# An encoder layer's down projection: staggered by sequence over its last chunks, with its half switch bank by bank and layer norm 2 spread out

## The reference

```
hdn = dwconv_centred(x @ ffn_w_up, ffn_conv_w) + ffn_conv_b
gate, val = split(hdn, 2)                       # 2816 columns each
ffn = (silu(gate) * val) @ ffn_w_down           # 2816 -> 1024
y = layer_norm(ALPHA * x + ffn, ln2_g, ln2_b)   # over the 1024 channels
```

## Time and profile before

| | |
|---|---|
| median of three runs | 1607.79 us (1606.72 to 1609.69) |
| span of the profiled execution | 1607.6 us |
| the median less that span | 0.2 us |
| TensorE, matmuls | 1456.8 us busy, 91% of the span |
| VectorE | 934.6 us, 58% |
| ScalarE | 501.1 us, 31% |
| GpSimd | 495.5 us, 31% |
| chain of waits, by engine | TensorE 70%, VectorE 21%, ScalarE 3% |

### The profile page before, as it was taken

One profiled execution on the slowest core, in us unless ns is written; L12 is line 12 of the kernel. 1 busy time (PEld: TensorE's weight loads), 2 busy tenths in 40 slices (PEclk: granted clock), 3 DMA queues, 4 the chain that ended last, 5 costly groups with the idle time before them and its releaser, 6 DMA issues.

```text
span 1607.6 us, 20068 instructions
## 1 busy us (share of the span) xinstructions
PE 1456.8 (91%) x7078; PEld 1179.5 (73%) x7078; DVE 934.6 (58%) x1447; ACT 501.1 (31%) x906; POOL 495.5 (31%) x235
## 2 busy tenths in 40 slices
PE   7999999798898897889579999999999999996992
PEld 5777767686786786768348888888888888875871
DVE  4344458858859779669884444434444445258337
ACT  4333346155163263421252212222221211212125
POOL 4322212112112122025254434434433444533323
PEclk9999999899899998999889999999999999998996
DMA  7110101100101001001001111111111111111002
GB/s 225 40 40 27 40 14 32 40 14 32 26 14 44 13 27 45 1 27 53 26 13 48 44 52 52 39 52 52 39 52 52 43 49 52 42 50 34 31 14 105
DMA packets 44326, 68.18 MB, mean 42 GB/s; under 512 B 24048, under 2 KB 26736, under 8 KB 44272
## 3 DMA queue, kind: packets, MB, share of 16 engines
q1 hardware_dynamic: 43696, 66.46, 13.1%
q10 hardware_dynamic: 576, 1.05, 0.2%
HBM read 62.00 MB, written 5.51 MB: 42 GB/s over the span
## 4 chain that ended last, share of the span: by engine, by line
PE 70%; DVE 21%; issue 4%; ACT 3%; DMA 2%; DVEq 0%; SPq 0%; POOL 0%; ACTq 0%
PE banks L503 33%; PE banks L955 14%; PE banks L528 11%; DVE qkv L1539 2%; DVE outer L1605 1%; PE banks L636 1%; PE banks L792 1%; PE banks L872 1%; DVE mix L1846 1%; DVE mix L1775 1%; PE banks L658 1%; DVE inv L1608 1%; DVE d_n L1699 1%; PE banks L646 1%; DVE sum L1788 1%
## 5 line engine op out<-in xcount | busy, mean ns | idle before, releaser
L441 POOL TENSOR_TENSOR w_hi<-w_raw,one 128x1024 fp32r<-128x1024 f32 (+1 forms) x103 | 196.0, 1903 | 1030.5 <-PE banks L503 496.8
L503 PE MATMUL banks<-x_hi,w_hi 128*128 128x512 f32 (+1 forms) x912 | 366.5, 402 | 30.5 <-POOL x_lo L463 16.9
L503 PE MATMUL banks<-x_hi,w_lo 128*128 128x512 f32 (+1 forms) x912 | 358.8, 393 | 0.0
L503 PE MATMUL banks<-x_lo,w_hi 128*128 128x512 f32 (+1 forms) x912 | 358.8, 393 | 0.0
L1870 DVE SCALAR_TENSOR_TENSOR cv<-banks,fw,cv 128x511 f32<-128x511 f32 x176 | 131.9, 750 | 260.6 <-ACT cv L1331 252.8
L444 POOL TENSOR_TENSOR w_lo<-w_raw,w_hi 128x1024 fp32r<-128x1024 f32 (+1 forms) x103 | 263.7, 2560 | 8.1
L503 PEld LDWEIGHTS banks<-x_hi,w_hi 128*128 128x128 f32 (+1 forms) x912 | 172.8, 189 | 77.6 <-POOL x_lo L463 20.6
L503 PEld LDWEIGHTS banks<-x_lo,w_hi 128*128 128x128 f32 (+1 forms) x912 | 172.8, 189 | 37.8 <-issue 2.8
L503 PEld LDWEIGHTS banks<-x_hi,w_lo 128*128 128x128 f32 (+1 forms) x912 | 172.3, 189 | 38.0 <-issue 0.6
L1331 ACT ACTIVATE cv<-banks,fw_j 128x512 f32<-128x512 f32 x88 | 68.7, 780 | 333.6 <-PE banks L503 331.1
L955 PE MATMUL banks<-a_hi,w_hi 128*128 128x512 f32 x352 | 139.7, 397 | 18.8 <-DVE a_lo L1898 15.6
(11 more groups left out here) (226 smaller groups left out, 2143.4 us busy)
## 6 DMA issues: line engine op xcount, KB each, us to landing
w_raw<-w_all SPq DMA_DIRECT2D x102, 512.0 KB, 3.3
yT<-z_all SPq DMA_DIRECT2D x16, 256.0 KB, 2.0
mix<-xT SPq DMA_DIRECT2D x12, 256.0 KB, 8.0
bw<-rpb SPq DMA_DIRECT2D x8, 132.5 KB, 12.0
mix<-xT ACTq DMA_DIRECT2D x4, 256.0 KB, 5.9
inverse_dram<-inv SPq DMA_DIRECT2D x4, 256.0 KB, 2.2
packed<-inverse_dram SPq DMA_DIRECT2D x16, 64.0 KB, 2.6
cst<-consts SPq DMA_DIRECT2D x1, 848.0 KB, 10.6
```

The source lines that it names most:

```text
L441: nc.gpsimd.tensor_tensor(w_hi[u][:, 0:n], w_raw[ru][:, 0:n], one[:, :].to_broadcast([P, n]), ALU.mult).then_inc(w_high, 1)
L503: last = mm(ps[bank][0:cols, :], w[u][:, k * cols:(k + 1) * cols], seq(x[:, k, :], s), start=n == 0, stop=n == 3 * KT - 1)
```

## The change

The first half keeps its order up to c10. The rest is rewritten:

- **Half switch.** c10 waits for both of its tiles and then finishes bank by bank (`half_finished`); VectorE reads each bank when it is done. The shift is summed from banks 0 and 1, after the first four banks. The two tiles of c11 stand in buffers of their own, in a part of `x_lo` that is no longer needed, since all rejoining of x (`joined`) is now done within the first half.
- **Moves.** A turn of the loop over c12 to c17 handles two chunks, and after each chunk's two `low` stands one group of four operations (`moved`): subtract the shift, scale block m + 4, add to the sum, add the square.
- **Stagger.** c18 to c21 (`STAG` = 4) are done for sequence 0 alone, all eight tiles, and then for sequence 1 bank by bank. All eight tiles' two parts (`h_last`, `l_last`) and four chunks' weights stay in memory for it; c20 and c21 have weight buffers of their own, for which GpSimd waits for no product. Sequence 0's sums (`stats2(0)`) stand after the first bank of sequence 1.
- **Layer norm 2.** Sequence 0's normalising is spread between the additions for sequence 1. The last tile of sequence 1 goes into the sums by matmuls of its own. The inverse root and the scaled mean that VectorE multiplies by stand in the PSUM banks `ps[4 + s]` and `ps[6 + s]`; GpSimd has copies in SBUF (`rs_row`, `mu_row`).

```diff
+        for u in range(2):
+            a_hi.append(x_lo[:, 2 * u, :])
+            a_lo.append(x_lo[:, 2 * u + 1, :])
...
+        h_last, late = place("h_last", [P, 2 * STAG, T], F32R, m)
+        w_late = []
+        for u in range(2):
+            t, late = place(f"w_hi_late{u}", [P, D], F32R, late)
+            t2, late = place(f"w_lo_late{u}", [P, D], F32R, late)
+            w_late.append((t, t2))
+        sq_last, late = place("sq_last", [P, L], F32, late)
+        rs_row, late = place("rs_row", [P, SEQS, L], F32, late)
+        assert late <= m + 2 * LONG * T * 4
+        l_last, _ = place("l_last", [P, 2 * STAG, T], F32R, m + 2 * LONG * T * 4)
...
-            split_chunks(UP0 + 3, CHUNKS)
+            split_chunks(UP0 + 3, DOWN0 + DPASS + 1)
+            split_chunks(DOWN0 + DPASS + 1, CHUNKS - 2, 6)
+
+            pool.wait_ge(a_ready, FJ + 12)
+            for u in range(2):
+                c = CHUNKS - 2 + u
+                split(c, raw(c), 3 + u, 16 * (c // 2 + 1), None)
...
+            def half_finished(c, w):
+                pe.wait_ge(w_ready, c + 1)
+                pe.wait_ge(a_ready, FJ)
+                for m in range(4):
+                    for s in range(SEQS):
+                        for t in range(2):
+                            ins = down_products(m, s, w, t, a_hi[t], a_lo[t], False, t == 1)
+                        ins.then_inc(proj_done, 1)
+                    if m == 1:
+                        pe.wait_ge(acc_read, SEQS)
+                        for s in range(SEQS):
+                            mm(ps[s][:, :], mean_w[:, :], seq(z_all[:, 0, :], s), start=True, stop=True
+                               ).then_inc(shift_summed2, 1)
...
+                pe.wait_ge(summed2, 2)
+                mm(ps[1][:, :], mean_w[:, :], sum2[:, 1, :], start=True, stop=False)
+                pe.wait_ge(sq_added2, 1 + 15)
+                mm(ps[3][:, :], mean_w[:, :], sumsq2[:, 1, :], start=True, stop=False)
+                pe.wait_ge(d_ready2, 16)
+                mm(ps[1][:, :], mean_w[:, :], seq(z_all[:, KT - 1, :], 1), start=False, stop=True)
+                pe.wait_ge(sq_last_ready, 1)
+                mm(ps[3][:, :], mean_w[:, :], sq_last[:, :], start=False, stop=True).then_inc(stats_done2, 1)
...
+            late = [(c0 + LONG + e, slot(c0 + LONG + e) if e < 2 else 1 + e) for e in range(STAG)]
+            for e, (c, w) in enumerate(late):
+                pe.wait_ge(w_ready, c + 1)
+                for t in range(2):
+                    n = 2 * e + t
+                    pe.wait_ge(a_ready, FJ + 2 * LONG + n + 1)
+                    for m in range(4):
+                        ins = down_products(m, 0, w, t, h_last[:, n, :], l_last[:, n, :], False, n == 2 * STAG - 1)
+                        if n == 2 * STAG - 1:
+                            ins.then_inc(proj_done, 1)
+            for m in range(4):
+                for e, (c, w) in enumerate(late):
                     for t in range(2):
+                        n = 2 * e + t
+                        ins = down_products(m, 1, w, t, h_last[:, n, :], l_last[:, n, :], False, n == 2 * STAG - 1)
+                ins.then_inc(proj_done, 1)
+                if m == 0:
+                    stats2(0)
+            stats2(1)
...
+            def root_rows(s):
+                act_e.wait_ge(stats_done2, s + 1)
+                A(sum2[:, s, :], ps[s][:, :], ACT.Square).then_inc(mean_squared, 1)
+                act_e.wait_ge(var_ready2, s + 1)
+                A(sumsq2[:, s, :], sumsq2[:, s, :], ACT.Ln, bias=eps[:, 2:3]).then_inc(ln_step2, 1)
+                act_e.wait_ge(ln_step2, s + 1)
+                A(rs_row[:, s, :], sumsq2[:, s, :], ACT.Exp, scale=-0.5).then_inc(rs_rows2, 1)
+                A(ps[4 + s][:, :], sumsq2[:, s, :], ACT.Exp, scale=-0.5).then_inc(rs_banked, 1)
+                act_e.wait_ge(mu_banked, s + 1)
+                nc.scalar.copy(mu_row[:, s, :], ps[6 + s][:, :]).then_inc(rows2_ready, 1)
...
+            def moved(m, s, n):
+                zt = tile_of(z_all, m, s)
+                TT(zt, zt, c2[:, s, :], ALU.subtract).then_inc(d_ready2, 1)
+                zt = tile_of(z_all, m + 4, s)
+                step(STT(zt, zt, ALPHA, c2[:, s, :], ALU.mult, ALU.subtract))
                 dve.wait_ge(d_ready2, n + 1)
-                return TT(sum2[:, s, :], sum2[:, s, :], tile_of(z_all, m, s), ALU.add)
+                step(TT(sum2[:, s, :], sum2[:, s, :], tile_of(z_all, m, s), ALU.add))
+                add_square2(n, s, s)
 
...
+            with dve.Fori(0, 3) as i:
+                step.enter(i, 2 * SEQS, base)
                 for s in range(SEQS):
+                    for u in range(2):
+                        t = 2 + 2 * s + u
+                        low(4 * i + (FJ + t), 4 * i + t, u)
+                    moved(i, s, 2 * i + s)
+            step.leave(3)
+            for n in range(2 * STAG):
+                dve.wait_ge(a_high, FJ + 2 * LONG + n + 1)
+                TT(l_last[:, n, :], act[:, 2 * LONG + n, :], h_last[:, n, :].bitcast(F32), ALU.subtract
+                   ).then_inc(a_ready, 1)
+                if n in (1, 3):
+                    moved(3, n // 2, 6 + n // 2)
...
+            def rows(s):
+                dve.wait_ge(mean_squared, s + 1)
+                TT(sumsq2[:, s, :], ps[2 + s][:, :], sum2[:, s, :], ALU.subtract).then_inc(var_ready2, 1)
+                dve.wait_ge(rs_rows2, s + 1)
+                TT(ps[6 + s][:, :], ps[s][:, :], rs_row[:, s, :], ALU.mult).then_inc(mu_banked, 1)
+                dve.wait_ge(mu_banked, s + 1)
+                dve.wait_ge(rs_banked, s + 1)
+            def normalised2(k, s):
+                zt = seq(z_all[:, k, :], s)
+                step(TT(zt, zt, ps[4 + s][:, :], ALU.mult))
+                if k == 0:
+                    dve.wait_ge(rows2_ready, s + 1)
...
+            for m in range(4):
+                completed(m, 0)
+            for m in range(4):
+                add2(m, 0)
+            for m in range(4):
+                add_square2(8 + m, 0, m % 2)
+            completed(0, 1)
+            add2(0, 1)
+            add_square2(12, 1, 0)
+            rows(0)
+            for k in range(KT):
+                if k not in POOL_TILES:
+                    normalised2(k, 0)
+                if k in (1, 4):
+                    m = 1 if k == 1 else 2
+                    completed(m, 1)
+                    add2(m, 1)
+                    add_square2(12 + m, 1, m % 2)
+            completed(3, 1)
+            rows(1)
+            for k in range(KT):
+                if k not in POOL_TILES:
+                    normalised2(k, 1)
```

More of the change, by code:

```diff
@@ L231, in encoder_layer @@
         w_lo.append(t)
+        for t, t2 in w_late:
+            w_hi.append(t)
+            w_lo.append(t2)
         banks = ctx.enter_context(nc.psum_tensor("banks", [P, 8, 512], F32))
@@ L448, in split_one, with split_chunks @@
                 split(c, raw(c), slot(c), 16 * (c // 2 + 1), free)
-            def split_chunks(first, end):
+            def split_chunks(first, end, more=0):
                 if (end - first) % 2:
-                    split_one(first, 2 * first - 2)
+                    split_one(first, 2 * first - 2 + more)
                     first += 1
@@ L457, in split_chunks @@
                         c = first + u
[L458 removed]
+                        split(2 * i + c, raw(c), slot(c), 16 * i + 16 * (c // 2 + 1), 4 * i + (2 * c - 2 + more))
             def low_x1(s):
@@ L950, in _, with down_products @@
                 up(j)
-            def down_products(m, s, t, u, start, stop):
-                for n, (w, a) in enumerate(((w_hi, a_hi), (w_hi, a_lo), (w_lo, a_hi))):
-                    ins = mm(ps[2 * m + s][:, :], w[u][:, t * 512 + m * P:t * 512 + (m + 1) * P],
-                             seq(a[t], s), start=start and n == 0, stop=stop and n == 2)
+            def down_products(m, s, w, t, hi, lo, start, stop):
+                for n, (wt, x) in enumerate(((w_hi, hi), (w_hi, lo), (w_lo, hi))):
+                    ins = mm(ps[2 * m + s][:, :], wt[w][:, t * 512 + m * P:t * 512 + (m + 1) * P],
+                             seq(x, s), start=start and n == 0, stop=stop and n == 2)
@@ new lines, in down @@
+                    b = 2 + t if first == 1 else t
+                    starts = first is not None and t == 0
+                    for m in (2, 3, 0, 1) if starts and first == 0 else range(4):
+                        if starts and first == 0 and m < 2:
+                            pe.wait_ge(up_conv, 4 * FJ - 2 + 2 * m)
+                        for s in range(SEQS):
+                            if starts and first == 1:
+                                if m:
+                                    pe.wait_ge(acc_read, 2 * m + s + 1)
+                                else:
+                                    pe.wait_ge(shift_copied2, s + 1)
+                            ins = down_products(m, s, w, t, a_hi[b], a_lo[b], starts, False)
@@ new lines, in _ @@
+            c0 = DOWN0
```

(30 more changed lines are left out.)

219 lines of the change are left out of this document (81 added, 138 removed).

## The result

The changed kernel takes 1588.04 us (median of 4 runs, 1587.09 to 1589.90); the kernel before, run beside it, 1607.26 us (4 runs, 1606.51 to 1609.69). The ratio is 0.9879, with a 95% interval of 0.9867 to 0.9891: 19 us faster. The forecast was 1582 us, in a range of 1571 to 1592. The sign and the range held; the size fell short by 6 us.

The account below looks back on a forecast made before the run. TensorE, busy for nine tenths of the span, was taken to bound the kernel; -10.4 us on TensorE and -15.1 in the tail made -25.5 from a span of 1607.6, so 1582 us was forecast, range 1571 to 1592.

Parts of the forecast that it names:

- Half switch: At c10 and c11: 3.1 us of new idle time ahead of c10, c11 following without a wait, 1.2 us gained.
- Moves: At c12 to c17: 10.88 us per chunk, the two stalls and the clock they cost gone, 17.8 us gained.
- Stagger: In c18 to c21: VectorE and GpSimd taking turns delay `l_last` 2 and 4; sequence 0's pass loses 9.1 us.
- so I take nothing: At c10: no loss of TensorE's clock was counted behind the 3.1 us wait, taken as nearer to 2.29 us.
- the other end of the bound: At c10: a clock loss of up to 2.5 us behind the wait, what c13 lost beside its own wait.
- tail: Layer norm 2 behind the last product: 24.5 us instead of 39.6, a gain of 15.1 us.
- The Trainium skill's rule on PSUM sources: Tail: 120 cycles fixed cost for PSUM against 58 for SBUF, adding an estimated 1.5 us; not used in the sum.
- no turns in the stagger: Rival, c18 to c21: VectorE's chain slips in ahead of GpSimd, up to 9.1 us come back, 1573 us; chance 0.14.
- The overlap is only partly had: Rival, sequence 0's tail under sequence 1's products: up to 15.1 us of gain lost, 1588 to 1600 us; chance 0.17.
- the clock at c10: Possible clock loss behind c10's wait, named as ending in the partial-overlap rival's stretch, from 1588 us up.
- The clock stays low: Rival, c18 to c21: TensorE stays at 1.2 GHz, costing up to 38 us more, all slow 1620 us; chance 0.03.
- it does nothing: Rival, c12 to c21: VectorE's chain, not TensorE, carries them, stalls only move, time stays at 1608 us; chance 0.02.

Follow-up runs that it names:

- e8: Changed kernel with c10's first tile multiplied for all banks, then its second bank by bank, still waiting for both tiles first: 1588.70 us, ratio 0.9880.
- e1: Changed kernel with c10 starting on its first tile for all banks once that is ready, then its second bank by bank: 1582.60 us, ratio 0.9843.
- e5: Kernel before with only the moves regrouped, one group in each chunk c12 to c19 instead of two every other chunk: 1591.34 us, ratio 0.9893.
- e7: Changed kernel with c10's first tile started first and moves 6 and 7 behind all `l_last` tiles: 1572.88 us, ratio 0.9784.
- e6: Changed kernel with VectorE using layer norm 2's rows in SBUF instead of the copies in PSUM: 1591.65 us, ratio 0.9893.
- e2: Changed kernel with moves 6 and 7 placed behind all eight `l_last` tiles instead of between them: 1579.05 us, ratio 0.9820.
- e3: Changed kernel without GpSimd's splits of c20's and c21's weights, their tiles multiplied with c18's and c19's weights: 1578.04 us, ratio 0.9811.

## Why the prediction was nearly right, and what was off

By spans, with the 1.7 us of scatter taken out, the change brought 20.5 us where 25.5 were forecast. The five missing us, place by place:

- **Half switch: 3.0 us too little taken.** 16.0 us were forecast from c9's end to behind the shift sums; the window shows 19.0. The idle time was right (3.1; measured 3.2). The step that failed is "so I take nothing", for the clock behind the wait: 14 products at 0.43 us cost 2.9 us of the 3.0, and even the other end of the bound (2.5) was short. e8 and e1 show that the wait, and not the order, brings this. The switch, forecast at -1.2 us, cost 1.8.
- **Moves: right.** c12 to c17 ran at full clock with no wait for `a_lo`. e5 measured 16.3 us for this part alone; the forecast had 17.8.
- **Stagger: the mechanism right, 1.0 us too little taken.** 30.9 us were forecast for sequence 0's pass and 32.0 passed. `l_last` 2 was used 8.6 us after c17's end, not 10.9: one operation of move 6 (1503.75) got in ahead of GpSimd's split, so there was one turn fewer and the wait was 3.2 us, not 5.5. `l_last` 4 came after 19.6 us (forecast 20.0): the missing turn came back in move 7, where two operations were drawn out (2.38 and 2.88 us) and not one, so that all six of GpSimd's operations were waited out as forecast and the error in the first wait did not reach the time. The slow products between the two waits cost nothing, as the forecast said; the eight behind the second wait were not in it.
- **Statistics between products** took 2.6 us, not 2.2, and the **tail** 25.1, not 24.5. In it, the last two sums (two matmuls each) ran at a granted clock of 0.54, some 0.85 us from one matmul to the next; the same sums in e7, at 1.00, are done 1.0 us sooner.
- **Around the span**, 1.8 us lie in each run of after, and not 0.2. With as much around it, the profiled execution of before was slower than the median run (1607.6 and 1.8 against 1607.79), and the forecast set its span against that median. A span of 1582.1 is a time of 1583.9.

The Trainium skill's rule on PSUM sources (VectorE: DVE Perf Modes, the section on the TRN2 errata), weighed in the prediction, isn't borne out: undisturbed tile operations take 0.68 and 0.69 us with one operand in a bank in the changed kernel, and 0.69 with both in SBUF in e6.

Of the rivals, "no turns in the stagger" did not happen, but its price was right: e2 and e3 get back 9.0 and 10.0 us, where up to 9.1 were forecast. "The overlap is only partly had" names the time that came (1588) by way of "the clock at c10"; its main mechanism, the tail, was nearly all had (0.6 us short). That 1588 lay in its range is luck in this respect. "The clock stays low" did not happen: the pass averages 0.89. Nor did "it does nothing": the stalls of c12 to c17 are gone and did not come back elsewhere at their old size.

Not settled: why the last sums of the changed kernel run at the low clock and those of e7 do not, behind the same idle time of 2.11 us.

## What to carry to other kernels

Price a wait of TensorE at what it stands still plus the slow products that may follow it: at c10 3.2 us of waiting cost 6, and starting on the half of the operands that was ready took nearly all of it back. When VectorE and GpSimd both work out of SBUF, count the VectorE operations that stand ahead of the one which TensorE wants: each may wait out a whole operation of GpSimd, so what is due goes first and what is not behind it. Before a stage is overlapped with another, find the one event from which the end follows (here sequence 0's sums); only what brings that event forward counts.
